# Filter spectra formed as two half sums, joined in the gate stage of a two-block transformer kernel

## The reference, cut to what matters

```python
def fft_long_conv(u, k_spec, skip):
    L = u.shape[1]
    uf = u.astype(jnp.float32)
    y = jnp.fft.irfft(jnp.fft.rfft(uf, n=2 * L, axis=1) * k_spec[None], n=2 * L, axis=1)[:, :L]
    return (y + uf * skip.astype(jnp.float32)).astype(u.dtype)

def hyena(z, conv_w, conv_b, w1, b1, w2, b2, freq, w3, skip):
    z = short_conv(z, conv_w, conv_b)
    v, x1, x2 = jnp.split(z, HY_ORDER + 1, axis=-1)
    filt = hyena_filters(z.shape[1], w1, b1, w2, b2, freq, w3)
    y = v
    for n, gate in enumerate((x1, x2)):
        k_spec = two_sided_spectrum(filt[:, 0, n], filt[:, 1, n])
        y = gate * fft_long_conv(y, k_spec, skip[n])
    return y
```

## Time and profile before

| what | value |
|---|---|
| median of 3 runs | 2633.13 us (2633.02 to 2635.64) |
| the profiled execution | 2630.96 us, its span 2629.6 us |
| PE busy | 2597.2 us (99%) |
| DVE busy | 1845.6 us (70%) |
| ACT busy | 1289.7 us (49%) |
| mean granted clock of TensorE | 0.997 |

### The profile page before, as it was taken

How to read it: one execution, slowest core, us unless ns; L and a number is a source line. 1 busy time by engine, 2 the same in 40 slices (tenths; PEclk the granted TensorE clock), 3 DMA queues, 4 the chain that set the end, 5 groups by cost and what they waited for, 6 DMA issues and landing times.

```text
span 2629.6 us, 31620 instructions
## 1 busy us (share of the span) xinstructions
PE 2597.2 (99%) x12546; PEld 2169.0 (82%) x12546; DVE 1845.6 (70%) x1927; ACT 1289.7 (49%) x1566; POOL 32.1 (1%) x55
## 2 busy tenths in 40 slices
PE   7999999999999999999999999999999999999999
PEld 3789988878888888888888888888888888988887
DVE  9978989988876644687776767756554665666565
ACT  2455444444444444555555544444444654545463
POOL 0000000000000000000000000000000000000000
PEclk9999999999999999999999999999999999999999
DMA  9998877798688755666555665555655556634554
GB/s 399 382 371 303 305 283 286 273 338 315 238 297 283 247 185 188 193 204 203 192 192 193 192 191 177 192 190 184 211 192 192 183 185 172 177 125 160 192 177 143
DMA packets 276584, 598.65 MB, mean 228 GB/s; under 512 B 21264, under 2 KB 46288, under 8 KB 260064
## 3 DMA queue, kind: packets, MB, share of 16 engines
q1 hardware_dynamic: 268272, 566.52, 63.2%
q0 software_dynamic: 4560, 21.56, 2.5%
q10 hardware_dynamic: 3616, 8.68, 0.8%
HBM read 586.24 MB, written 10.49 MB: 227 GB/s over the span
## 4 chain that ended last, share of the span: by engine, by line
PE 89%; DVE 7%; DMA 2%; issue 1%; ACT 1%; ACTq 0%; DVEq 0%; SPq 0%
PE ps L951 26%; PE ps L953 26%; PE ps L952 26%; DVE group_acc L2390 2%; PE ps L1076 2%; DVE w_lo L2271 2%; PE ps L1060 2%; PE ps L1063 1%; PE ps L1062 1%; DMA raw<-in_k_in 1%; PE ps L1461 1%; PE ps L1463 1%; PE ps L1462 1%; DMA raw<-in_w_in 1%; DVE ada_acc L2299 1%
## 5 line engine op out<-in xcount | busy, mean ns | idle before, releaser
L2271 DVE TENSOR_TENSOR w_lo<-raw,w_hi 128x1024 fp32r<-128x1024 f32 x870 | 1050.3, 1221 | 663.0 <-ACT w_hi L1607 661.0
L1607 ACT CAST w_hi<-raw 128x1024 fp32r<-128x1024 f32 x870 | 906.8, 1051 | 1074.5 <-PE ps L953 900.2
L951 PE MATMUL ps<-w_lo,x_hi 128*128 128x512 f32 x2592 | 1019.5, 393 | 6.6 <-DVE w_lo L2271 2.8
L953 PE MATMUL ps<-w_hi,x_lo 128*128 128x512 f32 x2592 | 1010.7, 390 | 0.0
L952 PE MATMUL ps<-w_hi,x_hi 128*128 128x512 f32 x2592 | 1010.0, 390 | 0.0
L951 PEld LDWEIGHTS ps<-w_lo,x_hi 128*128 128x128 f32 x2592 | 487.4, 188 | 111.9 <-DVE w_lo L2271 4.6
L953 PEld LDWEIGHTS ps<-w_hi,x_lo 128*128 128x128 f32 x2592 | 487.1, 188 | 102.1
L952 PEld LDWEIGHTS ps<-w_hi,x_hi 128*128 128x128 f32 x2592 | 487.6, 188 | 99.8 <-issue 1.0
L2299 DVE SCALAR_TENSOR_TENSOR ada_acc<-raw,cond,ada_acc 128x2048 f32<-128x2048 f32 x64 | 150.1, 2345 | 2.5 <-DMA raw<-in_w_ada 1.5
L951 PE MATMUL ps<-w_lo,pooled_hi 128*128 128x512 f32 x384 | 150.3, 391 | 0.0
L953 PE MATMUL ps<-w_hi,pooled_lo 128*128 128x512 f32 x384 | 149.5, 389 | 0.0
(11 more groups left out here) (379 smaller groups left out, 2135.9 us busy)
## 6 DMA issues: line engine op xcount, KB each, us to landing
raw<-in_w_m SPq DMA_DIRECT2D x128, 1024.0 KB, 5.2
raw<-in_w_ada SPq DMA_DIRECT2D x64, 1024.0 KB, 6.0
raw<-in_pool_w_in SPq DMA_DIRECT2D x64, 1024.0 KB, 5.3
raw<-in_w_in SPq DMA_DIRECT2D x56, 1024.0 KB, 7.3
raw<-in_k_mod SPq DMA_DIRECT2D x32, 1024.0 KB, 7.3
raw<-in_pool_w_out SPq DMA_DIRECT2D x32, 1024.0 KB, 5.0
raw<-in_ple_w_gate SPq DMA_DIRECT2D x32, 1024.0 KB, 5.1
raw<-in_mla_w_in SPq DMA_DIRECT2D x24, 1024.0 KB, 5.1
```

Of the source, the lines that this page charges most:

```text
L951: mm(bank, xh, wl, start=start, stop=False)
L953: ins = mm(bank, xl, wh, start=False, stop=stop)
L1607: nc.scalar.copy(by_ktile(st, w_hi[st.half_slot(j, half)][:, 0:n]), raw_half(st, j, half)).then_inc(hi_split, 1)
L2271: tt(by_ktile(st, w_lo[slot][:, 0:n]), raw_half(st, j, half), by_ktile(st, w_hi[slot][:, 0:n].bitcast(F32)), ALU.subtract).then_inc(lo_spl ...
```

## The change

Each spectrum is no longer formed for both frequency tiles. For the first frequency tile alone the even tokens' part and the odd tokens' part go to a PSUM bank each: 2 products instead of 4. In the gate stage DVE makes the two frequency tiles from them, `even + odd` and the difference, in place in `spec`, before the multiplication: `filter_low` ahead of half 9 and `filter_high` ahead of half 10 of each round. The wait for the loaded spectrum moves with it from half 13 to half 9. The forward table in SBUF shrinks to the first frequency tile, the inverse one to 128 rows, so both loads are 256 KB instead of 512 KB, and the rounding and splitting of the inverse table handle 512 columns instead of 1024. Nothing else changes place.

```diff
-        sync.dma_start(dft[:, 0:2].rearrange("p m t n -> p (m t n)"), a["k_dft"][0]).then_inc(dft_in, 16)
+        sync.dma_start(dft_f[:].rearrange("p m t n -> p (m t n)"), a["k_dft_f"]).then_inc(dft_in, 16)
...
-        pool.dma_start(dft[:, 2:4].rearrange("p m t n -> p (m t n)"), a["k_dft"][1]).then_inc(tables_in, 16)
+        pool.dma_start(dft_i[:].rearrange("p m n -> p (m n)"), a["k_dft_i"]).then_inc(tables_in, 16)
...
         def spectrum(it, m):
             pe.wait_ge(filt_win, 2 * it + m + 1)
-            for f in range(2):
-                for t in range(2):
-                    ins = mm(ps[:, spec_bank(it, m) + f, :], dft[:, m, t, f * P:(f + 1) * P],
-                             (h_sum, h_dif)[m][:, t, :], start=t == 0, stop=t == 1)
+            for t in range(2):
+                ins = mm(ps[:, spec_bank(it, m) + (1 - t if m else t), :], dft_f[:, m, t, :], (h_sum, h_dif)[m][:, t, :],
+                         start=True, stop=True)
             ins.then_inc(spec_mm, 1)
...
-            part = slice(0, S if m else P)
-            nc.scalar.copy(dft_hi[:, m:m + 2, :, part], dft[:, m:m + 2, :, part]).then_inc(dft_round, 1)
+            hi, src = (dft_i_hi, dft_i) if m else (dft_f_hi, dft_f)
+            nc.scalar.copy(hi[:], src[:]).then_inc(dft_round, 1)
...
+        def filter_low(n):
+
+            dve.wait_ge(spec_in, 16 * (n + 1))
+            then(tt(spec[:, 0:4:2], spec[:, 0:4:2], spec[:, 1:4:2], ALU.add))
+
+        def filter_high(n):
+
+            then(stt(out=spec[:, 1:4:2], in0=spec[:, 1:4:2], scalar=-2.0, in1=spec[:, 0:4:2], op0=ALU.mult, op1=ALU.add))
+
         def multiply_re(n):
 
-            dve.wait_ge(spec_in, 16 * (n + 1))
...
-            run_at(st, i, {4: lambda: in_g(i, 0), 8: lambda: signal_rest(i), 12: lambda: in_g(i, 1),
+            run_at(st, i, {4: lambda: in_g(i, 0), 8: lambda: signal_rest(i), 9: lambda: filter_low(i),
+                           10: lambda: filter_high(i), 12: lambda: in_g(i, 1),
```

More of the change, by code:

```diff
@@ L50 @@
           "b_m1", "pre_norm_2", "ple_norm_2", "pool_scale_2", "mla_q_norm_2",
-          "mla_kv_norm_2", "positions_2", "k_feats")
+          "mla_kv_norm_2", "positions_2", "k_feats", "k_dft")
 def tables():
@@ L108, in laid_out @@
         "k_w3": np.concatenate([w3[:, 0:2 * W1], w3[:, 2 * W1:4 * W1]]),
-        "k_dft": a["k_dft"].reshape(2, 2, 2, P, S).transpose(0, 3, 1, 2, 4).reshape(2, P, 4 * S),
+        "k_dft_f": a["k_dft"][0:2, :, 0:P].reshape(2, 2, P, P).transpose(2, 0, 1, 3).reshape(P, 2 * S),
+        "k_dft_i": a["k_dft"][2:4, 0:P].transpose(1, 0, 2).reshape(P, 2 * S),
         "k_window": a["k_window"].reshape(2, P, 2, CH).transpose(2, 1, 0, 3).reshape(2, P, 2 * CH),
@@ L249, in block_kernel @@
     group_acc = [at(f"group_acc{i}", 112 + 4 * i, [2 * CH]) for i in range(2)]
-    dft = at("dft", 128, [4, 2, S])
+    dft_f = at("dft_f", 128, [2, 2, P])
+    dft_i = at("dft_i", 132, [2, S])
     sgu_wT = at("sgu_wT", 136, [8, P])
@@ L277, in block_kernel @@
     prod_lo = [at("prod_lo0", 144, [2, CH], F32R), at("prod_lo1", 140, [2, CH], F32R)]
-    dft_hi = at("dft_hi", 190, [4, 2, S], F32R)
-    dft_lo = at("dft_lo", 128, [4, 2, S], F32R)
+    dft_f_hi = at("dft_f_hi", 190, [2, 2, P], F32R)
+    dft_f_lo = at("dft_f_lo", 128, [2, 2, P], F32R)
+    dft_i_hi = at("dft_i_hi", 194, [2, S], F32R)
+    dft_i_lo = at("dft_i_lo", 132, [2, S], F32R)
     spec = at("spec", 136, [4, CH])
@@ L1243, in forward @@
                     bank = ps[:, 4 + 2 * m + t, :]
-                    mm(bank, dft_hi[:, m, t, 0:P], hy_lo[:, t, :], start=True, stop=False)
-                    mm(bank, dft_hi[:, m, t, 0:P], hy_hi[:, t, :], start=False, stop=False)
-                    ins = mm(bank, dft_lo[:, m, t, 0:P], hy_hi[:, t, :], start=False, stop=True)
+                    mm(bank, dft_f_hi[:, m, t, :], hy_lo[:, t, :], start=True, stop=False)
+                    mm(bank, dft_f_hi[:, m, t, :], hy_hi[:, t, :], start=False, stop=False)
+                    ins = mm(bank, dft_f_lo[:, m, t, :], hy_hi[:, t, :], start=False, stop=True)
             ins.then_inc(hy_f, 1)
@@ L1254, in inverse @@
                     part = 1 - t if m else t
-                    mm(bank, dft_lo[:, 2 + m, 0, tokens], prod_hi[m][:, part, :], start=m == 0, stop=False)
-                    mm(bank, dft_hi[:, 2 + m, 0, tokens], prod_hi[m][:, part, :], start=False, stop=False)
-                    ins = mm(bank, dft_hi[:, 2 + m, 0, tokens], prod_lo[m][:, part, :], start=False, stop=m == 1)
+                    mm(bank, dft_i_lo[:, m, tokens], prod_hi[m][:, part, :], start=m == 0, stop=False)
+                    mm(bank, dft_i_hi[:, m, tokens], prod_hi[m][:, part, :], start=False, stop=False)
+                    ins = mm(bank, dft_i_hi[:, m, tokens], prod_lo[m][:, part, :], start=False, stop=m == 1)
             ins.then_inc(inv_mm, 1)
@@ L2537, in split_dft @@
             dve.wait_ge(dft_round, m // 2 + 1)
-            part = slice(0, S if m else P)
-            tt(dft_lo[:, m:m + 2, :, part], dft[:, m:m + 2, :, part], dft_hi[:, m:m + 2, :, part].bitcast(F32),
-               ALU.subtract).then_inc(dft_split, 1)
+            lo, src, hi = (dft_i_lo, dft_i, dft_i_hi) if m else (dft_f_lo, dft_f, dft_f_hi)
+            tt(lo[:], src[:], hi[:].bitcast(F32), ALU.subtract).then_inc(dft_split, 1)
         def moments(src, width, t):
```

## The result

The changed kernel takes 2639.45 us (median of 10 runs) where the kernel before takes 2633.84 us (10 runs beside it): a ratio of 1.0023, 95% interval 1.0014 to 1.0032. The ratio makes 6.1 us, the two medians differ by 5.6: both come from the same runs, worked out in two ways. The forecast was 2638.2 us, in a range of 2633.5 to 2641.5. The profiled execution took 2638.36 us, with a span of 2637.1.

What follows compares the result with a forecast made beforehand. The first stage was taken to wait for DVE and transfers, the gate stage to be led by PE with DVE close behind. +5.2 us there less 0.1 for the first, on 2633.13, gave 2638.2 us, range 2633.5 to 2641.5.

Steps and rivals of the forecast that it cites:

- Part 1: First stage: halving eight spectra saves PE 14.4 us, taken as 0 on the span because PE waits for DVE.
- Part 2: Gate stage: two added DVE instructions take 1.25 and 1.31 us start to start, 2.56 us a round, 10.2 us in all.
- Round 0: Gate stage, first round: DVE waits for ACT ahead of halves 9 to 11, so both new instructions fit; cost 0.
- Round 1: Gate stage: `gate_out` 1.76 us late, half 12 1.30 late, so PE loses 1.2 us at half 14.
- Round 2: Gate stage: the 1.30 us carry over, loads being as late as DVE; PE 3.0 us late in sum at half 14.
- Round 3: Gate stage: DVE enters 3.0 us late and adds 2.56 with little idle; half 14 on PE 5.2 us late in sum.
- The sum: Whole kernel: +5.2 us from the gate stage less 0.1 for the first stage, so +5.1 us.
- The spectrum's load: Gate stage: the load lands by 383.2 us, `filter_low` comes at 389.6; 6 us of room, cost 0.
- Rival 1: Gate stage: DVE catches up between rounds, so about no change, 2633.1 to 2635.5 us; chance 0.17.
- Rival 2: First stage does shorten as PE's sums end sooner and transfers run ahead; at full effect 2623.9 us; chance 0.07.
- Rival 3: PE's clock falls behind waits of about 2.3 us ahead of half 14, rounds 2 and 3; 2639.9 us; chance 0.15.
- Rival 4: Gate stage: strided operands or a collision with transfers cost 0.5 us more an instruction, to 2641 us; chance 0.05.

## Why the prediction was right, and where it was not

**Part 1, the halved spectra: 0 us.** Right in size. The join left out, and the join made early, are both at the time of before. PE waits for DVE's sum at the end of the stage as it did, since the 14.4 us went into waits and into a lower clock. The prediction said what would show it: an idle time ahead of 113.76 grown by 10 us or more, and an end that stays. The end stayed within its scatter. PE's idle time ahead of that half (now at 115.87) grew from 19.0 to 28.7 us, by 9.6, of which 2.1 are its later arrival; without the fall of the clock it would have grown by more. That fall is a step that I missed: I priced a fall ahead of 113.76 and found it covered by PE's later wait, but asked only what PE's halves would lose. The fall lay at 57 us, and what it delayed was a sum for which DVE waits, the engine that bounds the stage: 0.8 to 1.8 us each time. In the comparisons of whole kernels it is too small to be told from nothing, so the size of the term stands by luck as much as by working. A second effect of the missing products, at 439 us, is told under round 2. In the sum, part 1 stands with 0.1 us gained, though I had set it at 0; no row gives this 0.1.

**Part 2, price of the instructions.** `filter_low` was to take 1224 ns and takes 1.22 us. `filter_high` was to take 1283 ns, from the earlier trace rows, and takes 1.22 as well: it reads no per-partition scalar, as the row I took it from does. Whether this makes the difference no run shows. The blocks that lie apart cost nothing extra.

**Round 0: 0.** The number can't be read apart from scatter, since all counting starts from there. **Round 1: 1.2.** Measured 1.2, 1.1 and 1.0 in the three profiles (the working gives 411.52 - 410.40 = 1.1, and I wrote 1.2). The way was right too: `gate_out` 1.81 late where 1.76 was said, half 12 1.35 where 1.30 was said, on the timeline above.

**Round 2: 3.0 in sum.** Measured 3.9, 3.8 and 4.1: this is the term that was mis-sized. What comes on top is a wait that the trace of before had not shown at this place (timeline of DVE, after, ahead of half 8 of round 2):

```profile
435.62 2.34 DVE L2302 SCALAR_TENSOR_TENSOR ada_acc<-raw,cond,ada_acc 128x2048 f32<-128x2048 f32 x1
439.03 2.35 DVE L2302 SCALAR_TENSOR_TENSOR ada_acc<-raw,cond,ada_acc 128x2048 f32<-128x2048 f32 x1 [1.06 <-DMA raw<-in_w_ada]
```

DVE waits for the transfer of `w_ada`, and `gate_out` of round 2 is 4.1 us late where I had 3.1. Of the waits in this round I had said that DVE comes late by the same as its loads, so that none would grow; this one did. It is 1.1 to 1.3 us in the three profiles of the changed kernel, and at most 0.2 in both of the kernel before and both with every product made twice. The latter's rounds 2 and 3 fit the prediction's 3.0 and 5.2, with 2.9 and 4.9, 3.0 and 5.4.

The wait does not come from the join. It stands at 1.0 to 1.3 us in the three profiles without a join in the gate stage (where 0.3 to 0.7 us of it reach half 14), at 1.13 with the join in round 1 alone, at 1.4 and 1.0 with two spectra's products made twice, and at 0.4 at least with the join on POOL. So it is in all ten profiles of kernels with fewer products in the first stage than before, and in none of the four with all of them. Thus the failed step is in part 1: of the 6.0 us in the gate stage about 0.9 come from the halved spectra, for which I had taken 0, and the 5.2 of the join agree with the 4.9 and 5.4 measured where all products are made.

How can products missing before 90 us make a load late at 439? The issue of the loads does not tell: 46.2 us behind round 0's half 14 in both profiles of before, 47.5 after the change, but 47.4 and 47.6 with all products made twice, without the wait. One thing does move with the number of products, a load of 16 KB in a queue of kind `instruction` (DMA view of 427 to 431 us after the change, and of 416 to 420 us before):

```profile
q8 instruction: 1, 0.02, 1.6%
...
raw<-in_w_ada SPq DMA_DIRECT2D x1, 1024.0 KB, 11.9
```

```profile
q8 instruction: 1, 0.02, 1.5%
```

In the four profiles without the wait it comes 58 to 59 us behind round 0's half 14, some 7 us ahead of the issue of the last `w_ada`; in the other ten it comes at 66 to 69 us, 0.7 to 1.9 us behind this issue. The slowest load of `raw` in this part of the stage lands 10.7 to 11.1 us after its issue in the four and 11.9 to 12.4 in the ten. That the one load holds up the other is a conclusion from these fourteen profiles; no run moved it by itself, and it is not shown.

**Round 3: 5.2 in sum.** Measured 6.0, 5.8 and 6.2, the 0.9 of round 2 carried on; round 3 itself adds about 2.1, and 2.2 were said. **The sum**, +5.1, is measured at +5.6 by the medians and +6.1 by the ratio. That it is so near is in part luck: the 0.9 us were not foreseen, and the first stage scatters by more than that.

**The spectrum's load** was not waited for by DVE in any round. Right.

**Rival 1** (DVE catches up) is refuted by the join in round 1 alone. **Rival 2** (the first stage shortens) is refuted by the join left out. **Rival 3** (the clock): its place was wrong. The waits at half 14 of rounds 2 and 3 were 1.65 us, not 2.3, since part of the loss now falls on half 13 (0.93 and 0.53 us, where PE had not waited before), and the granted clock behind them stayed at 1.00:

```profile
467.00:474.00 7.00, 6.37 (x27) 4.94 (x28) 6.96 (x9) 4.19 (x5) 0.00 (x0) 1.00 0.35 108
...
522.00:530.00 8.00, 8.00 (x37) 6.62 (x36) 7.97 (x9) 4.96 (x5) 0.00 (x0) 1.00 0.49 136
```

I looked for a fall only where I had already found a wait, and not in the first stage, where the change itself takes PE's work away. **Rival 4** (the operands, a collision) is not there with the join on DVE; the join on POOL shows what a collision looks like.

## To carry to other kernels

Work taken from an engine that waits in a stage gives nothing, and work given to an engine at 93% in another costs its full length less only what idle time lies ahead of the point where the bound engine needs it; so read the waits in order of time, not their sum (11.8 us of idle took up only 5 of the 10.2 us added). The join cost nothing measurable where it stood on the same engine, in a stage in which that engine has room, once, before the value is stored. To tell what work added in one place costs, compare kernels that are alike in the other: here a wait at 439 us went with products left out before 90. And take two or three profiles before a shift of a microsecond is called an effect: two of the same kernel differed by 3.4 us at the same instruction.

## What the runs showed of the hardware that I had not expected

Taking PE's products away lowered its clock for the work left: at 30 to 40 us the granted clock went from 0.83 to 0.57 (with all products made twice it was 0.71 and 0.83), and sixteen one-column products took 3.54 us where they had taken 1.92 (timelines of PE, after and before):

```profile
33.32 3.54 PE L1128 MATMUL ps<-ones,group_acc 128*128 128x1 f32 x16 [6.04 <-DVE group_acc L2393]
```

```profile
33.21 1.92 PE L1125 MATMUL ps<-ones,group_acc 128*128 128x1 f32 x16 [2.75 <-DVE group_acc L2390]
```

0.50 in the row of 57 to 61 us is the lower of the two levels, 1.2 GHz. Making two spectra's products twice brings back the full clock at 57 us, and the time is not measurably changed by it.

The fall at 326 to 332 us, which costs 1.6 us, has no wait of PE ahead of it but a row of one-column products. These alone do not bring it each time: that it stayed away in both profiles of one kernel, with the same work around it, I could not explain.

Of the scatter between executions of one kernel a part goes with TensorE's clock: 5 us between a mean granted clock of 0.994 and of 0.997.

POOL's `tensor_tensor` of 128x1024 float32 values takes 3.0 to 3.4 us in the mean, against 1.22 on DVE, and DVE's instructions with two or three operands in SBUF take 40% to 100% longer where it runs (6.74 us for 4.80, 6.26 for 3.5, 948 ns for 480).

A load of 16 KB for instructions stood 66 to 69 us behind round 0's half 14 in ten profiles and 58 to 59 us in four, by the number of products far ahead of it, and a load of weights landed about 1 us later in the ten.
